# Two transposes of the routing four units later, and the exponential two units earlier, in a one-core transformer kernel

## The chip, the cores and the metric

The kernel is one launch on one core of a Trainium2 chip. The metric is device time in microseconds of that core. A core has five engines with a program of their own each, which meet only through semaphores: TensorE (PE in the profile), VectorE (DVE), ScalarE (ACT), GpSimd (POOL) and SyncE (SP), which here only issues the loads.

## The reference, cut to what matters

Two blocks run one after the other on 256 tokens of width 1024: a transformer block with two layers, then a block with a state-space branch, an attention branch and a PEER layer, all in fp32. The change is in the PEER layer. It is:

```
q = (x @ w_q)                       # 8 heads, 2 halves of 128
s1, s2 = q . sub_k1, q . sub_k2     # 128 scores per head and half
v1, i1 = top_k(s1, 16); v2, i2 = top_k(s2, 16)
cand_s = v1[..., :, None] + v2[..., None, :]        # 16 x 16
top_s, pos = top_k(cand_s, 16)
experts = (i1 * 128 + i2) at pos;  gates = softmax(top_s)
act = gelu(u_tab[experts] . x) * gates
out = sum_e act * v_tab[experts]
```

There are 128 x 128 experts and each token takes 8 x 16 of them.

## The kernel before, in words

The kernel does not gather experts. It computes the hidden value of every expert for every token, multiplies it with a gate that is zero where the token did not choose the expert, and multiplies the result with the whole second table. The first table is streamed as 128 *expert units* (stage `ut`, 512 KB each, 128 experts), the second as 128 more (stage `vt`).

A weight tile of fp32 is split in two halves so that TensorE's faster number format can be used with three products: ScalarE copies the tile to `wh` (L845), and VectorE or GpSimd subtracts to get `wl` (L1121, L1709). Which of the two does it stands in the list `lower`: for `ut` it is GpSimd below the unit `J_GATE` and VectorE from there on. There are four slots, so a unit's halves can be made only when the unit four before it has been used by TensorE. At its place j each engine's program makes the half of unit j + 3 at the latest (`stream`, `until`).

The order of work is written out by hand, as a loop over j from 0 to 127 in each engine's program:

- **TensorE**: `hidden(j)`, 24 products of 128 x 256, into one of four banks. Ahead of unit 25 and of unit 51 (`J_SEL`) stands `sel_turned(t)` (L782): it waits until VectorE has finished the routing of token tile t (event `picked`) and transposes three tiles, gates (`gt`) and the two chosen indices (`sel`), into bank 2 or 3. From `J_GATE` = 53 on, for 64 units, `gates_of(j - J_GATE)` (L791) adds, for four tokens each, the product of two one-hot matrices: the gates of four tokens for all experts.
- **ScalarE**: the exponential of `gt` of tile t ahead of its unit 25 or 51 (it waits for the event `top`), then `wh`, then the Gelu of `hidden(j)`; in the gate phase also a copy of gates into `H` for the units that are still to come.
- **VectorE**: `routing(t)` (L1594) is a generator that is moved on by one step at each j, by two where j % 5 is 4: 16 steps of a top-16 over 128 scores, 8 of a top-16 over 256 sums, the subtraction that gives `top`, index arithmetic, four wide operations and two sums over 128 x 2048, and the softmax's last product (`picked`). At j = 25 and 51 what is left of it is done at once, then `sel_turned(t)` (L1626) copies the transposed tiles from the bank, then the next tile's routing starts. From j = 53 on it makes the one-hot matrices (`one_hots`), nine in rotation, multiplies the gates into `H` for the units already computed (`gates_in`, width 4 x (J_GATE + g + 1)), and gates the new unit (`gated_hidden`).
- **GpSimd**: only `wl`.

Each call `wait_ge` in this code issues an instruction only if the engine has not met that value already.

Of the kernel before, what the change touches and what calls it, by code (L numbers as in the profile page):

```python
# [95 lines left out]
def program(nc, x_d, pos_d, consts_d, smalls_d, win_d, wout_d, wup_d, wdown_d, rows_d, wu_d, wqkv_d, wqk_d, wga_d, wsm_d,  # L96
            wglu_d, wsu_d, wau_d, wout2_d, wpq_d, keys_d, ut_d, vt_d, out_d, spill_d):
    with ExitStack() as ctx:
# [51 lines left out]
        def signal(name, step=1):  # L150
            return Signal(ctx.enter_context(nc.semaphore(name)), name, step)

        pe_out, act_out, dve_out, pool_out = [signal(n) for n in ("pe_out", "act_out", "dve_out", "pool_out")]
# [57 lines left out]


        J_SEL = (25, 51)
        J_GATE, N_GR = 53, 64


        lower = []
# [157 lines left out]
        def RT(n):  # L375
            r_at[0] += n
            assert r_at[0] <= 32768
            return H_s[:, r_at[0] - n:r_at[0]]
# [12 lines left out]
        sel = RT(256).rearrange("p (a n) -> p a n", a=2)  # L391
# [9 lines left out]
        def gate_bank(g):  # L401
            return (2, 3, 6, 7)[g % 4]

        def hid_bank(j):
            return (0, 1, 4, 5)[j % 4]

        def gated_before(j):
            return min(max(j - J_GATE, 0), N_GR)
# [36 lines left out]
        def pe(p):  # L445
# [7 lines left out]
            def claim(b):  # L453
                if emptied[b]:
                    p.wait_ge(emptied[b][0], *emptied[b][1:])
# [318 lines left out]
            def hidden(j):  # L774
                i, b = first["ut"] + j, hid_bank(j)
                unit(i)
                claim(b)
                m = mm3(banks[b][:, 0:256], [unit_pair(i, k, 8, tcols(0)) for k in range(8)], [hT(k, ALLC) for k in range(8)], True, True, ready_both(("f", 2)))
                m.then_inc(pe_out.up(("used", i), ("hid", j)), 1)
                emptied[b] = (dve_out, ("HG", j)) if gated_before(j) else (act_out, ("H", j))  # L780

            def sel_turned(t):  # L782
                b = 2 + t
                claim(b)
                p.wait_ge(dve_out, ("picked", t))
                for j, src in enumerate((gt.rearrange("p h k -> p (h k)"), sel[:, 0, :], sel[:, 1, :])):
                    m = p.e.transpose(banks[b][:, j * 128:(j + 1) * 128], src, ids[:, :])
                m.then_inc(pe_out.up(("sel", t)), 1)
                emptied[b] = (dve_out, ("selG", t))

            def gates_of(g):  # L791
                b = gate_bank(g)
                claim(b)
                for t in range(4):
                    k = 4 * g + t
                    p.wait_ge(dve_out, ("oh", k))
                    o = oneh[k % N_OH]
                    mm(banks[b][:, t * 128:(t + 1) * 128], [(o[:, 0, :], o[:, 1, :])]
                       ).then_inc(pe_out.up(("Gt", k), ("G", g) if t == 3 else None), 1)
                emptied[b] = (dve_out, ("G", g))  # L800
# [17 lines left out]
                                m.then_inc(pe_out.up(("Vend", t)), 1)  # L818

            for j in range(128):  # L820
                if j in J_SEL:
                    sel_turned(J_SEL.index(j))
                hidden(j)
                if 0 <= j - J_GATE < N_GR:
                    gates_of(j - J_GATE)
# [5 lines left out]
        def act(a):  # L831
# [5 lines left out]
            def stream(i):  # L837
                while at[0] <= until[i]:
                    u = at[0]
                    at[0] += 1  # L840
                    if plan[u][2]:
                        a.wait_ge(slot_in[slot[u]], ("raw", u))
                        if halves_of[u] is not None:
                            a.wait_ge(pe_out, ("used", halves_of[u]))
                        a.e.activation(high_of(u), raw_of(u), ACTF.Copy).then_inc(act_hi.up(("hi", u)), 1)  # L845

            def do(out, src, f, ev, **kw):
                a.e.activation(out, src, f, **kw).then_inc(act_out.up(ev), 1)  # L848
# [218 lines left out]
            stream(first["keys"])  # L1067
            stream(first["keys"] + 1)
            for j in range(128):
                if j in J_SEL:  # L1070
                    t = J_SEL.index(j)
                    a.wait_ge(dve_out, ("top", t))
                    do(gt, gt, ACTF.Exp, ("gt", t))
                stream(first["ut"] + j)

                n, b = 4 * gated_before(j), hid_bank(j)
                a.wait_ge(pe_out, ("hid", j))
                if j * 256 + 256 > R_AT:
                    a.wait_ge(dve_out, ("selG", 1))
                if n < 256:  # L1080
                    do(H[:, j, n:256], banks[b][:, n:256], ACTF.Gelu_apprx_tanh, ("H", j))
                if n:
                    do(banks[b][:, 0:n], banks[b][:, 0:n], ACTF.Gelu_apprx_tanh, ("H", j))
                g = j - J_GATE
                if 0 <= g < N_GR:
                    a.wait_ge(pe_out, ("G", g))
                    do(H[:, j + 1:128, 4 * g:4 * g + 4], banks[gate_bank(g)][:, :].rearrange("p (t j) -> p j t", t=4)[:, j + 1:128, :],
                       ACTF.Copy, ("Gs", g))
# [23 lines left out]
        def dve(v):  # L1112
# [11 lines left out]
            def tt(out, a, b, op, ev=None, alone=False):  # L1124
                if not alone:
                    v.wait_ge(dve_out)
                v.e.tensor_tensor(out, a, b, op).then_inc(dve_out.up(ev), 1)  # L1127
# [177 lines left out]
            for L in range(DEPTH):  # L1305
# [76 lines left out]
                for n in range(2):  # L1382
                    for h in range(4):
                        if h in (0, 3):
                            t = h // 3
# [155 lines left out]
            for c in range(20):  # L1541
# [4 lines left out]
                if c - 4 in (7, 15):  # L1546
                    t = (c - 4) // 8
# [9 lines left out]
            for n in range(2):  # L1557
                for h in range(4):
                    if h in (0, 3):
                        t = h // 3  # L1560
# [33 lines left out]
            def routing(t):  # L1594
                v.wait_ge(act_out, ("S", t, 12))
                for n in range(16):
                    top16(v16[:, n, :], i16[:, n, :], S[:, t, n, :])
                    yield
                vv = v16.rearrange("p (h c) k -> p h c k", c=2)
                tt(cand.rearrange("p h (i j) -> p h i j", i=16), vv[:, :, 0, :].unsqueeze(3).broadcast_to([128, 8, 16, 16]),  # L1600
                   vv[:, :, 1, :].unsqueeze(2).broadcast_to([128, 8, 16, 16]), ALU.add)
                for h in range(8):
                    top16(tops[:, h, :], pos[:, h, :], cand[:, h, :])
                    yield
                tt(gt, tops, tops[:, :, 0:1].broadcast_to([128, 8, 16]), ALU.subtract, ("top", t))
                posf_ = pos.rearrange("p h k -> p (h k)")
                ts(pau, posf_, 4, None, ALU.logical_shift_right, None)
                ts(pbu, posf_, 15, None, ALU.bitwise_and, None)
                copy(pa, pau)
                copy(pb, pbu)  # L1610
                copy(if16, i16)
                yield
                ifv = if16.rearrange("p (h c) k -> p h c k", c=2)
                for c, pp in ((0, pa), (1, pb)):
                    tt(oh, pp.rearrange("p (h k) -> p h k", h=8).unsqueeze(3).broadcast_to([128, 8, 16, 16]),
                       iot.unsqueeze(1).unsqueeze(1).broadcast_to([128, 8, 16, 16]), ALU.is_equal)
                    yield
                    tt(oh, oh, ifv[:, :, c, :].unsqueeze(2).broadcast_to([128, 8, 16, 16]), ALU.mult)
                    reduce_sum(sel[:, c, :].rearrange("p (h k) -> p h k", h=8), oh)
                    yield  # L1620
                v.wait_ge(act_out, ("gt", t))
                reduce_sum(zs, gt)
                reciprocal(zs, zs)
                tt(gt, gt, zs.unsqueeze(2).broadcast_to([128, 8, 16]), ALU.mult, ("picked", t))

            def sel_turned(t):  # L1626
                bank = banks[2 + t]
                v.wait_ge(pe_out, ("sel", t))
                v.wait_ge(spilled, "spill")
                copy(sel1[:, tcols(t)], bank[:, 128:256])  # L1630
                copy(sel2[:, tcols(t)], bank[:, 256:384])
                copy(selG[:, tcols(t)], bank[:, 0:128], ("selG", t))
# [24 lines left out]
            for j in range(128):  # L1657
                if j in J_SEL:
                    for _ in steps:
                        pass  # L1660
                    sel_turned(J_SEL.index(j))
                    steps = routing(1) if j == J_SEL[0] else iter(())
                next(steps, None)
                if j % 5 == 4:
                    next(steps, None)
                g = j - J_GATE
                if 0 <= g < N_GR:
                    one_hots(g)
                stream(first["ut"] + j - (g >= 0))
                if 0 < g <= N_GR:  # L1670
                    gates_in(g - 1)
                gated_hidden(j - 1)
# [310 lines left out]
```

## Time and profile before

| | |
|---|---|
| Median of 3 runs | 1963.02 us (1962.67 to 1963.16) |
| The profiled execution | 1962.71 us, of which 1960.6 us is the span from its first to its last instruction |
| TensorE busy | 1785.2 us (91%) |
| VectorE busy | 1281.3 us (65%) |
| ScalarE busy | 868.9 us (44%) |
| GpSimd busy | 779.2 us (40%) |
| Mean granted TensorE clock | 0.925 |

The profile is of one execution. A line such as "PE bank L468" in it names an engine, the tile that is written and the line of the program; "idle before" is the time that the engine stood still ahead of the instruction, and the arrow names what released it. Because helpers issue most instructions, L468 stands for nearly all products, L787 for the six transposes of `sel_turned`, L848 for ScalarE's functions, L1127 for VectorE's operations on two tensors. The routing of the PEER layer lies between about 1155 and 1320 us of the span, its gate phase between about 1331 and 1566 us, and the second table after about 1597 us.

### The profile page before, as it was taken

Reading aid. Unit: us, or ns where it says so; the run is one execution under the profiler, and the core shown is the slowest. Engines: PE = TensorE matmul, PEld = TensorE weight load, DVE = VectorE, ACT = ScalarE, POOL = GpSimd, SP = SyncE. Lnnn points to the kernel's source line nnn. Section 1 sums busy time; section 2 is a strip of 40 time slices with the busy share of each in tenths; the row PEclk is TensorE's granted clock in tenths of the full one; section 3 lists DMA queues with packets and bytes.
Section 4 is the critical chain, followed back from the end, with each engine's and each line's share of the span. In section 5 each row is a group of like instructions: output and inputs, shape, how many; then the busy total and the mean of one; then the engine's idle time right before and its main releaser. Section 6 shows DMA issues by size and latency. Waiting matters only on the chain.

```text
span 1960.6 us, 27291 instructions
## 1 busy us (share of the span) xinstructions
PE 1785.2 (91%) x10680; PEld 1555.1 (79%) x10680; DVE 1281.3 (65%) x2470; ACT 868.9 (44%) x1500; POOL 779.2 (40%) x410
## 2 busy tenths in 40 slices
PE   5999899789989997688889899789999999999997
PEld 4677899677669996555667799789999988888886
DVE  6653674954546758687763459998999944444444
ACT  5443565335336652412432344444444445555553
POOL 3211468432125683175633359770000014444443
PEclk9887899899789998788967899899999999999998
DMA  6421455444115554322321535454444456666664
GB/s 219 140 76 33 167 179 192 145 175 133 54 36 201 181 175 161 132 76 76 105 77 54 179 127 182 149 166 142 144 141 141 149 170 193 194 195 193 194 192 141
DMA packets 77311, 283.19 MB, mean 144 GB/s; under 512 B 8704, under 2 KB 8960, under 8 KB 76800
## 3 DMA queue, kind: packets, MB, share of 16 engines
q1 hardware_dynamic: 75888, 275.97, 43.3%
q10 hardware_dynamic: 1296, 5.49, 0.7%
q8 instruction: 84, 1.38, 0.3%
q14 instruction: 43, 0.35, 0.1%
HBM read 279.33 MB, written 2.10 MB: 144 GB/s over the span
## 4 chain that ended last, share of the span: by engine, by line
PE 64%; DVE 24%; ACT 4%; issue 4%; POOL 3%; DMA 1%; POOLq 0%; DVEq 0%; ACTq 0%
PE bank L468 52%; PE bank L459 9%; DVE wl L1121 4%; DVE tab L1127 2%; DVE H L1127 2%; ACT wh L845 2%; PE bank L551 2%; DVE att L1132 2%; DVE ssb L1127 1%; DVE att L1138 1%; DVE H L1586 1%; DVE H L1592 1%; DVE H L1588 1%; DVE H L1584 1%; DVE H L1590 1%
## 5 line engine op out<-in xcount | busy, mean ns | idle before, releaser
L1709 POOL TENSOR_TENSOR wl<-raw,wh 128x1024 fp32r<-128x1024 f32 x231 | 598.9, 2602 | 862.3 <-ACT wh L845 862.1
L845 ACT ACTIVATE wh<-raw 128x1024 fp32r<-128x1024 f32 x515 | 531.4, 1048 | 175.4 <-PE bank L468 166.0
L468 PE MATMUL bank<-hh,wh 128*128 128x256 f32 x1904 | 545.6, 287 | 18.6 <-DVE hl L1127 17.3
L468 PE MATMUL bank<-hl,wh 128*128 128x256 f32 x1904 | 538.1, 283 | 0.0
L468 PE MATMUL bank<-hh,wl 128*128 128x256 f32 x1904 | 536.8, 282 | 0.0
L1121 DVE TENSOR_TENSOR wl<-raw,wh 128x1024 fp32r<-128x1024 f32 x284 | 402.7, 1426 | 131.0 <-ACT wh L845 130.8
L468 PEld LDWEIGHTS bank<-hh,wh 128*128 128x128 f32 x1904 | 364.4, 191 | 20.9 <-issue 14.4
L468 PEld LDWEIGHTS bank<-hl,wh 128*128 128x128 f32 x1904 | 364.3, 191 | 0.0
L468 PEld LDWEIGHTS bank<-hh,wl 128*128 128x128 f32 x1904 | 363.8, 191 | 0.0
L1127 DVE TENSOR_TENSOR acl<-H,ach 128x256 fp32r<-128x256 f32 x128 | 87.6, 685 | 183.2 <-ACT ach L848 183.2
L468 PE MATMUL bank<-wh,ach 128*128 128x512 f32 x512 | 200.0, 391 | 1.9 <-DVE acl L1127 1.9
L468 PE MATMUL bank<-wl,ach 128*128 128x512 f32 x512 | 199.9, 390 | 0.0
L468 PE MATMUL bank<-wh,acl 128*128 128x512 f32 x512 | 199.7, 390 | 0.0
L468 PE MATMUL bank<-wh,hh 128*128 128x512 f32 (+1 forms) x432 | 184.3, 427 | 11.5 <-DVE hl L1127 6.6
L848 ACT ACTIVATE H<-bank 128x256 f32<-128x256 f32 (+33 forms) x193 | 63.8, 331 | 256.5 <-PE bank L468 224.0
L468 PE MATMUL bank<-wl,hh 128*128 128x512 f32 (+1 forms) x432 | 177.2, 410 | 0.0
L468 PE MATMUL bank<-wh,hl 128*128 128x512 f32 (+1 forms) x432 | 176.8, 409 | 0.0
L848 ACT ACTIVATE ach<-H 128x256 fp32r<-128x256 f32 x128 | 53.4, 418 | 174.3 <-PE bank L468 173.8
L1138 DVE SCALAR_TENSOR_TENSOR att<-bank,sml,att 128x255 f32<-128x255 f32 (+1 forms) x176 | 84.5, 480 | 64.0 <-ACT att L848 60.9
L468 PEld LDWEIGHTS bank<-wh,hh 128*128 128x128 f32 x432 | 88.1, 204 | 41.0 <-issue 15.2
L468 PEld LDWEIGHTS bank<-wh,ach 128*128 128x128 f32 x512 | 96.4, 188 | 22.3 <-issue 2.1
L468 PEld LDWEIGHTS bank<-wl,ach 128*128 128x128 f32 x512 | 96.5, 189 | 20.1
(183 smaller groups left out, 2439.5 us busy)
## 6 DMA issues: line engine op xcount, KB each, us to landing
raw<-in_ut_dram SPq DMA_DIRECT2D x128, 512.0 KB, 3.5
raw<-in_vt_dram SPq DMA_DIRECT2D x128, 512.0 KB, 3.6
raw<-in_wup_dram SPq DMA_DIRECT2D x88, 512.0 KB, 4.0
raw<-in_win_dram SPq DMA_DIRECT2D x48, 512.0 KB, 4.5
raw<-in_wdown_dram SPq DMA_DIRECT2D x44, 512.0 KB, 3.6
raw<-in_wout_dram SPq DMA_DIRECT2D x24, 512.0 KB, 3.5
raw<-in_wga_dram SPq DMA_DIRECT2D x16, 512.0 KB, 3.6
raw<-in_wpq_dram SPq DMA_DIRECT2D x16, 512.0 KB, 3.6
```

The lines of the kernel that those rows point to most:

```text
L459: m = p.e.matmul(out, l, r, start=i == 0, stop=i == len(pairs) - 1)
L468: m = p.e.matmul(out, lhs[i][a], rhs[i][b], start=start and i == 0 and j == 0, stop=stop and i == n - 1 and j == 2)
L551: m = p.e.transpose(banks[b][:, 128 * k:128 * k + 128], buf[:, 1024 + 256 * (i % NB) + 128 * k:1152 + 256 * (i % NB) + 128 * k], ids[:, :])
L845: a.e.activation(high_of(u), raw_of(u), ACTF.Copy).then_inc(act_hi.up(("hi", u)), 1)
L848: a.e.activation(out, src, f, **kw).then_inc(act_out.up(ev), 1)
L1121: v.e.tensor_tensor(low_of(u), raw_of(u), high_of(u).bitcast(F32), ALU.subtract).then_inc(dve_lo.up(("lo", u)), 1)
L1127: v.e.tensor_tensor(out, a, b, op).then_inc(dve_out.up(ev), 1)
L1132: v.e.tensor_scalar(out, a, s1, None, op0).then_inc(dve_out.up(ev), 1)
L1138: v.e.scalar_tensor_tensor(out, a, s, b, op0, op1).then_inc(dve_out.up(ev), 1)
L1584: v.e.max(values[:, 0:8], s_).then_inc(dve_out.up(), 1)
L1586: v.e.max_index(index[:, 0:8], values[:, 0:8], s_).then_inc(dve_out.up(), 1)
L1709: g.e.tensor_tensor(low_of(u), raw_of(u), high_of(u).bitcast(F32), ALU.subtract).then_inc(pool_lo.up(("lo", u)), 1)
```

## The change

In TensorE's and VectorE's loops `sel_turned(t)` stands at units 29 and 55 instead of 25 and 51, and the gate phase begins at unit 57 instead of 53 (so units 53 to 56 of `ut` are lowered by GpSimd, not VectorE, and `gates_in` is 16 elements wider each time). ScalarE's exponential stands at units 23 and 49 instead of 25 and 51. VectorE still finishes tile 0's routing and starts tile 1's at unit 25. A wait is written ahead of the subtraction that overwrites `gt`.

```
-        J_GATE, N_GR = 53, 64
+        J_TURN = (29, 55)
+        J_GATE, N_GR = 57, 64
 (TensorE)
-                if j in J_SEL:
-                    sel_turned(J_SEL.index(j))
+                if j in J_TURN:
+                    sel_turned(J_TURN.index(j))
                 hidden(j)
 (ScalarE)
-                if j in J_SEL:
-                    t = J_SEL.index(j)
+                if j + 2 in J_SEL:
+                    t = J_SEL.index(j + 2)
                     a.wait_ge(dve_out, ("top", t))
                     do(gt, gt, ACTF.Exp, ("gt", t))
 (VectorE, routing)
+                if t:
+                    v.wait_ge(pe_out, ("sel", t - 1))
                 tt(gt, tops, tops[:, :, 0:1].broadcast_to([128, 8, 16]), ALU.subtract, ("top", t))
 (VectorE, loop)
                 if j in J_SEL:
                     for _ in steps:
                         pass
-                    sel_turned(J_SEL.index(j))
                     steps = routing(1) if j == J_SEL[0] else iter(())
+                if j in J_TURN:
+                    sel_turned(J_TURN.index(j))
```

## Rows read from the trace of the kernel before

**Rows 1.** The page's chain that ended last, shares of the span by engine

```profile
PE 64%; DVE 24%; ACT 4%; issue 4%; POOL 3%; DMA 1%; POOLq 0%; DVEq 0%; ACTq 0%
```

**Rows 2.** Waits of TensorE, 1000 to 1700 us: total us, times, longest

```profile
PE bank L787 <- DVE H L1127: 18.0, 2, 10.0
```

**Rows 3.** TensorE in order of time (start us, us, what)

```profile
1237.14 0.87 PE L787 MATMUL bank<-ids,H 128*128 128x128 f32 x3 [9.96 <-DVE H L1127]
1237.67 0.56 PE L468 MATMUL bank<-hh,wh 128*128 128x256 f32 x1
...
1320.22 0.90 PE L787 MATMUL bank<-ids,H 128*128 128x128 f32 x3 [8.07 <-DVE H L1127]
1320.77 0.56 PE L468 MATMUL bank<-hh,wh 128*128 128x256 f32 x1
...
1326.04 0.34 PE L468 MATMUL bank<-hh,wh 128*128 128x256 f32 x1
```

**Rows 4.** Windows: stretch, us, busy PE, PEld, DVE, ACT, POOL; clock, DMA share, GB/s

```profile
1250.00:1312.00 62.00, 62.00 (x533) 61.94 (x531) 58.52 (x156) 29.33 (x44) 56.72 (x22) 1.00 0.56 179
1480.00:1520.00 40.00, 40.00 (x349) 40.00 (x348) 40.00 (x119) 18.12 (x44) 0.00 (x0) 1.00 0.41 137
```

**Rows 5.** ScalarE in order of time around its units 25 and 51

```profile
1227.22 0.38 ACT L848 ACTIVATE H<-bank 128x256 f32<-128x256 f32 x1 [1.46 <-PE bank L468]
1227.62 1.28 ACT L848 ACT_TABLE_LOAD   x1
...
1230.19 1.28 ACT L848 ACT_TABLE_LOAD   x1
1242.18 0.39 ACT L848 ACTIVATE H<-bank 128x256 f32<-128x256 f32 x1 [10.71 <-PE bank L468]
...
1312.18 0.38 ACT L848 ACTIVATE H<-bank 128x256 f32<-128x256 f32 x1 [1.47 <-PE bank L468]
...
1326.28 0.39 ACT L848 ACTIVATE H<-bank 128x256 f32<-128x256 f32 x1 [9.84 <-PE bank L468]
```

**Rows 6.** VectorE in order of time, both routings

```profile
1208.52 0.29 DVE L1127 TENSOR_TENSOR H<-H 128x128 f32<-128x128 f32 x1
...
1235.32 1.67 DVE L1127 TENSOR_TENSOR H<-H 128x128 f32<-128x128 f32 x1
1238.05 0.94 DVE L1143 COPY xs<-bank 128x128 f32<-128x128 f32 x3 [1.06 <-PE bank L787]
1239.03 0.29 DVE L1584 MAX8 H<-H 128x8 f32<-128x128 f32 x1
...
1268.55 2.29 DVE L1127 TENSOR_TENSOR H<-H 128x2048 f32<-128x2048 f32 x1
...
1290.95 0.29 DVE L1127 TENSOR_TENSOR H<-H 128x128 f32<-128x128 f32 x1
...
1319.87 0.29 DVE L1127 TENSOR_TENSOR H<-H 128x128 f32<-128x128 f32 x1
```

**Rows 7.** GpSimd in order of time: lower halves, one unit each

```profile
1225.80 4.39 POOL L1709 TENSOR_TENSOR wl<-raw,wh 128x1024 fp32r<-128x1024 f32 x1
1230.15 4.40 POOL L1709 TENSOR_TENSOR wl<-raw,wh 128x1024 fp32r<-128x1024 f32 x1
1234.51 2.34 POOL L1709 TENSOR_TENSOR wl<-raw,wh 128x1024 fp32r<-128x1024 f32 x1
...
1296.79 2.40 POOL L1709 TENSOR_TENSOR wl<-raw,wh 128x1024 fp32r<-128x1024 f32 x1 [0.32 <-ACT wh L845]
```

**Rows 8.** VectorE and TensorE in order of time, gate phase

```profile
1481.11 0.78 DVE L1127 TENSOR_TENSOR H<-H,bank 128x376 f32<-128x376 f32 x2
...
1561.79 0.36 PE L468 MATMUL bank<-hh,wh 128*128 128x256 f32 x1
...
1561.84 0.35 DVE L1641 TENSOR_SCALAR xs<-sta,xs 128x128 f32<-128x128 bf16 x1
...
1566.07 0.97 DVE L1127 TENSOR_TENSOR H<-H,bank 128x468 f32<-128x468 f32 x2 [0.74 <-ACT H L848]
```

## The prediction

> **What bounds the kernel now.** I read the page's chain first: TensorE carries 64% of it and VectorE 24% [rows 1], so a gain must come from time in which TensorE stands still or runs slow. The waits of TensorE in the last third then have one large entry: the transposes of `sel_turned` waited 18.0 us for VectorE, in two waits, the longer 10.0 us [rows 2]. In order of time these are 9.96 us ahead of unit 25 and 8.07 us ahead of unit 51 [rows 3]. Between them TensorE is busy 62.00 of 62 us at full granted clock [rows 4]: nothing else holds it.
>
> The true price of a stall is larger than its wait, since TensorE resumes at the low clock. ScalarE's Gelus follow TensorE's units, so their distance tells it. From Gelu 25 at 1242.18 to Gelu 50 at 1312.18 are 25 units in 70.0 us, 2.80 us each [rows 5]. Gelu 24 to Gelu 25 took 14.96 us, so stall 25 cost 12.16 us; Gelu 50 to Gelu 51 took 14.10, so stall 51 cost 11.30 us [rows 5]. Together 23.46 us. The slow part can be seen: unit 51 ran from 1320.77 to 1326.04, 5.27 us instead of 2.80 [rows 3], 2.5 us at 1.2 instead of 2.4 GHz for most of it; unit 25 started at 1237.67 [rows 3] and its Gelu came 4.5 us later [rows 5], so about 1.6 us.
>
> Why is VectorE late? Its routing of tile 1 starts at 1239.03 and its last product ends at 1319.87 + 0.29 = 1320.16 [rows 6]: 81.1 us of almost unbroken work. The 26 units of TensorE that are meant to cover it take 26 x 2.80 = 72.8 us. So VectorE's routing, not TensorE, sets when unit 51 starts, and that is the number on which the change has to be judged.
>
> **The change, first tile.** Tile 0's routing ends at 1235.32 + 1.67 = 1236.99 [rows 6]. Without the stall TensorE would go on after unit 24 (about 1226.95) with units 25 to 28, 11.2 us, to 1238.15, already past 1236.99. But GpSimd must have made their lower halves. In front of each of the last ones it takes turns with VectorE's wide operations: the three operations that start at 1225.80, 1230.15 and 1234.51 are the halves of units 26, 27 and 28, and end at 1230.19, 1234.55 and 1236.85 [rows 7] (the last one started before the stall ended belongs to unit 28, the last that `stream(25)` allows). Unit 26 would start at 1229.75 and so waits 0.4 us; unit 27 would start at 1233.0 and waits 1.6 us; unit 28 runs 1237.4 to 1240.2. So `sel_turned(0)` is reached at about 1240.2 and finds `picked` long set: no stall for VectorE, 2.0 us for GpSimd, and 0.5 us for the transposes themselves (1237.14 to 1237.67 [rows 3]). The two short waits may lower the clock for one unit, which costs 0 to 2.5 us by unit 51's row; I take 0. As shown next, it drops out of the sum in either case.
>
> **The change, second tile.** VectorE no longer stands for TensorE's transposes after tile 0 and starts tile 1 at 1237.0 instead of 1239.03, 2.04 us sooner. Its three copies (0.94 us [rows 6]) come at its unit 29, four steps into the routing; their transposes are then long done. So VectorE is 2.04 - 0.94 = 1.10 us ahead, and tile 1 is picked at about 1320.16 - 1.1 = 1319.1. TensorE runs from 1240.75 with units 29 to 54, 72.8 us, and reaches `sel_turned(1)` at 1313.5. It waits 5.6 us. This is where the first tile's 0 to 2.5 us vanish: they only shorten this wait. TensorE then pays transposes and a slow first unit as before; I take the same 2.5 us (bounds: 0, if the shorter idle leaves the clock up, and 2.5 as now, with 1.6 of unit 25 between).
>
> **The sum.** Before, unit 51 starts 0.61 us after `picked`, at 1320.77 [rows 3, 6]. After, unit 55 starts 0.6 us after `picked`, at about 1319.7. So at a moment 1.1 us earlier, four more units are done. All units, all 64 gate steps and all 128 units of the second table are still to be done in both, and TensorE was the bound in them, so the four units are the gain: 4 x 2.80 + 1.10 = 12.3 us. Counted from the other side: 23.46 us lost before, 2.0 + 0.5 + 5.6 + 0.6 + 2.5 = 11.2 us lost after, difference 12.3.
>
> **What costs nothing, and its cover.** The wait ahead of the `gt` subtraction: VectorE has met the same event in its own copies at unit 29, so it issues no instruction. The earlier exponential: at unit 23 `top` of tile 0 is set at 1208.81 [rows 6], over 10 us ahead; at unit 49 ScalarE comes at about 1296.9, and `top` of tile 1, 1291.24 less 1.1 [rows 6], is there 6 us before. What is queued behind it is the high half of unit 26 (52) and a Gelu. From the end of one Gelu at 1227.60 to the end of the second table load at 1231.47 ScalarE spends 3.87 us including one high half of about 1.05, so the exponential with its two loads costs 2.8 us [rows 5], now beside a running TensorE. ScalarE idles 1.47 us per unit [rows 5], so it is level again after two units, and the high half is four units ahead of its use. Price if the cover is gone: at most 2.8 us ahead of unit 29 or 55, again only taken from the waits there. The Trainium skill, "ScalarE: Activation LUTs", section "What ACT_TABLE_LOAD costs", gives a load of 1283 ns plus a drain of 1380 ns for every switch, and so speaks against moving the switches beside running work: an estimate of 5.6 us by it instead of 2.8. The trace has the load (1.28 us) but no drain ahead of it (Gelu ends 1227.60, load starts 1227.62), so the row is used; by the page's figure too the result would stay, as ScalarE's delay ends in the wait at unit 55.
>
> The gate phase: TensorE and VectorE are both busy 40.00 of 40 us in 1480 to 1520 [rows 4], so VectorE is close to taking over. `gates_in` grows by 16 elements a step. The pair of operations grew from 0.78 us (376 + 160 elements) to 0.97 (468 + 252) [rows 8], 1.03 ns an element; 64 x 16 x 1.03 = 1.06 us in all. VectorE's last one-hot of the phase ends at 1562.19, when TensorE has just begun the unit ahead of its last gate step (1561.79 + 2.8) [rows 8]: 2.4 us in hand, of which at most 1.06 goes. Cost 0; bounds 0 and 1. GpSimd lowers four units more (53 to 56) in time that it had free; VectorE saves them, but after the stall.
>
> **A size I can't fix: turns with GpSimd.** VectorE's wide operation took 2.29 us at 1268.55 [rows 6], and GpSimd's took 4.39 where both were wide and 2.34 to 2.40 alone [rows 7]. So one turn is worth about 2.1 us. In the new order tile 1's candidate sum comes within 0.1 us of GpSimd's next start, and the exponential delays GpSimd's unit 52 just where VectorE's wide operations begin (1296.9 [rows 7]). VectorE may lose or win a turn. A lost one at the candidate sum is mostly given back at the index arithmetic, which waits for the same GpSimd end. I take 0, and -2.1 and +2.8 us (one whole unit later) as ends.
>
> **The rivals.** (a) *Both stalls go*, 23.5 us, 1939.6 us: needs VectorE to route a tile in 72.8 us; it needs 81.1, and nothing of it is removed. 3%. (b) *VectorE wins a turn, or the clock stays up at unit 55*: 12.3 + 2.3, 1948.4 us. 13%. (c) *VectorE loses a turn in tile 1*: `picked` 2.8 us later, 1953.5 us. 13%. (d) *Little is gained*: the four units run, but GpSimd, which shares its turns with VectorE, holds TensorE for more than I count and pushes VectorE as well, three turns, 6 to 8 us: 1958. 4%. (e) *Slower*: VectorE becomes the bound of the gate phase. Its place is each of the 64 steps; it decides once VectorE's step is longer than TensorE's unit plus gates by over 12.3/64 = 0.19 us on the mean. The last steps are some 0.1 us longer now, so a strided write that costs more than its elements would be needed. At 0.25 us a step, 16 us, so 3.7 slower: 1966.7 us. 4%. (f) *It does not do what it says*: TensorE stands at unit 29 for something else as long as at 25: 1963. 3%.
>
> **How the numbers follow.** The forecast has 60%. Against the profiled execution, 1962.71 us (span 1960.6 and 2.11 around it), it is 1950.4; the median of the runs is 0.31 higher, so 1950.7 us. Its own range is 1949.2 to 1952.3. For 8 in 10 the range takes in (b) and (c): 1947.5 to 1954.5. A difference of 0.2% (4 us) is about what can be told here: faster 0.92 (forecast, a, b, c and most of d), same 0.04, slower 0.04.
>
> **What would show it.** No wait of the transposes at unit 29; short waits of TensorE for `wl` L1709 of 0.4 and 1.6 us near 1230 and 1233; one wait at unit 55 of 5 to 6 us for VectorE's last product, with low clock behind it; tile 1's routing starting at 1237; the gate phase still at TensorE's pace. It is wrong if unit 55 starts later than 1322, or if waits for one-hots appear in the gate phase.

## The result, and the profile after

| | before | after |
|---|---|---|
| Median of 20 runs each | 1961.13 us (1947.05 to 1971.12) | 1941.28 us (1931.87 to 1959.17) |
| Ratio of the runs | | 0.9927 (95%: 0.9900 to 0.9955) |
| The profiled execution | 1962.71 us, span 1960.6 | 1932.87 us, span 1930.8 |
| Mean granted clock | 0.925 | 0.938 |

The kernel is faster, and the predicted ratio, 1950.7 / 1963.02 = 0.9937, lies in the interval. The predicted time does not hold: the median is 9.4 us below it and 6.2 below the range. The ratios here and below leave out single runs over 1.5% above the fastest of their kernel, one each in three of the later comparisons. The two profiled executions differ by 29.8 us in span, far more than the 12.3 us of the prediction. So there are two questions: what did the change do, and where are the other 17 us?

The waits of TensorE in the last third, after the change (total us, times, longest), which answer to [rows 2]:

```profile
PE bank L788 <- DVE H L1128: 5.7, 1, 5.7
PE bank L469 <- POOL wl L1713: 2.9, 3, 1.3
PE bank L469 <- DVE acl L1128: 1.9, 1, 1.9
```

One wait for VectorE is left, 5.7 us; 5.6 was forecast. TensorE in order of time, which answers to [rows 3]: the unit that waits for GpSimd's half, the transposes of tile 1, and the first product of the second table.

```profile
1142.17 0.39 PE L469 MATMUL bank<-hh,wh 128*128 128x256 f32 x1 [1.28 <-POOL wl L1713]
...
1217.30 0.38 PE L469 MATMUL bank<-hh,wh 128*128 128x256 f32 x1 [1.32 <-POOL wl L1713]
...
1302.04 0.90 PE L788 MATMUL bank<-ids,H 128*128 128x128 f32 x3 [5.74 <-DVE H L1128]
1302.60 0.56 PE L469 MATMUL bank<-hh,wh 128*128 128x256 f32 x1
...
1568.72 0.47 PE L469 MATMUL bank<-wh,ach 128*128 128x512 f32 x1 [1.91 <-DVE acl L1128]
```

The first and the last row bound a stretch that can be compared: from unit 1, which in both kernels waits 1.28 us for its half, to the second table. It takes 1568.72 - 1142.17 = 426.55 us. In the kernel before these two rows are:

```profile
1159.43 0.39 PE L468 MATMUL bank<-hh,wh 128*128 128x256 f32 x1 [1.28 <-POOL wl L1709]
...
1598.44 0.47 PE L468 MATMUL bank<-wh,ach 128*128 128x512 f32 x1 [1.91 <-DVE acl L1127]
```

That is 439.01 us. The change took 12.46 us from the stretch it touches. The other 17.3 us were gained before unit 1 began, in code that is the same in both kernels: 15.7 of them in the attention steps of the first block's layer 0, and 1.8 in those of layer 1 (table below). Windows of the attention steps of the first block's layer 0 (stretch, us, busy PE, PEld, DVE, ACT, POOL, granted clock, DMA share, GB/s), first of before, then of after:

```profile
131.00:154.00 23.00, 23.00 (x79) 16.85 (x78) 9.43 (x41) 8.14 (x32) 2.50 (x2) 0.51 0.08 24
154.00:171.00 17.00, 16.44 (x66) 12.58 (x65) 6.34 (x19) 5.39 (x16) 0.00 (x0) 0.56 0.01 1
```

```profile
131.00:154.00 23.00, 21.64 (x137) 16.67 (x136) 13.80 (x57) 12.63 (x46) 1.08 (x2) 1.00 0.08 25
```

The column to read is the clock, 0.51 against 1.00: TensorE ran the same instructions at 1.2 GHz in the one execution and at 2.4 in the other, and got 79 or 137 of them done in 23 us. TensorE looks fully busy in the slow one, which is why a list of waits does not show this loss. The mean granted clock of the single runs goes with their time as well: among the 20 runs after the change it is 0.938 in the fastest (1931.87 us) and 0.923 in the slowest (1959.17 us).

### The profile page after: what moved, and what is told of

Read it like the earlier page. It is cut to its first block, busy times and chain, and to the rows that moved or that the text cites. A ratio compares the mean times of both kernels' runs of the same rounds, so it can differ in the third digit from the quotient of the medians.

```text
span 1930.8 us, 27287 instructions
## 1 busy us (share of the span) xinstructions
PE 1764.5 (91%) x10680; PEld 1540.3 (80%) x10680; DVE 1272.1 (66%) x2462; ACT 867.7 (45%) x1500; POOL 789.6 (41%) x414
## 3 DMA queue, kind: packets, MB, share of 16 engines
q8 instruction: 84, 1.38, 0.3%
## 4 chain that ended last, share of the span: by engine, by line
PE 63%; DVE 25%; ACT 4%; issue 4%; POOL 3%; DMA 1%; POOLq 0%; DVEq 0%; ACTq 0%
PE bank L469 52%; PE bank L460 8%; DVE wl L1122 4%; DVE tab L1128 2%; DVE H L1128 2%; ACT wh L846 2%; PE bank L552 2%; DVE att L1133 2%; DVE ssb L1128 1%; DVE att L1139 1%; DVE H L1587 1%; DVE H L1593 1%; DVE H L1589 1%; DVE H L1591 1%; DVE H L1585 1%
## 5 line engine op out<-in xcount | busy, mean ns | idle before, releaser
L1713 POOL TENSOR_TENSOR wl<-raw,wh 128x1024 fp32r<-128x1024 f32 x235 | 609.0, 2603 | 821.2 <-ACT wh L846 821.0
L469 PE MATMUL bank<-hh,wh 128*128 128x256 f32 x1904 | 546.0, 287 | 20.2 <-DVE hl L1128 17.3
L1122 DVE TENSOR_TENSOR wl<-raw,wh 128x1024 fp32r<-128x1024 f32 x280 | 396.3, 1423 | 129.2 <-ACT wh L846 129.0
L469 PEld LDWEIGHTS bank<-wl,ach 128*128 128x128 f32 x512 | 96.6, 189 | 20.2
```

The lines of the kernel that those rows point to most:

```text
L469: m = p.e.matmul(out, lhs[i][a], rhs[i][b], start=start and i == 0 and j == 0, stop=stop and i == n - 1 and j == 2)
L1122: v.e.tensor_tensor(low_of(u), raw_of(u), high_of(u).bitcast(F32), ALU.subtract).then_inc(dve_lo.up(("lo", u)), 1)
L1713: g.e.tensor_tensor(low_of(u), raw_of(u), high_of(u).bitcast(F32), ALU.subtract).then_inc(pool_lo.up(("lo", u)), 1)
```

## The experiments

For every profiled execution I read the same marks from TensorE's order. *Layer 0* is from its third group of q and k transposes to the transposes of the normed rows that wait 6.0 us; *layer 1* the same in the next layer; *stretch* is the one above. Each row is one profiled execution; the ratio is that of all its kernel's runs to runs of the kernel before in the same comparison.

| kernel | ratio (95%) | layer 0 | layer 1 | to unit 1 | stretch |
|---|---|---|---|---|---|
| before | | 88.3 | 88.7 | 1159.4 | 439.0 |
| before, look 1 | | 72.6 | 86.9 | 1140.1 | 436.7 |
| before, look 2 | | 88.3 | 88.6 | 1162.4 | 436.8 |
| before, look 3 | | 72.6 | 87.0 | 1147.0 | 436.5 |
| after | 0.9927 (0.9900 to 0.9955) | 72.6 | 86.9 | 1142.2 | 426.6 |
| after, again | 0.9936 (0.9908 to 0.9964) | 88.3 | 88.7 | 1159.5 | 425.7 |
| first move only | 0.9975 (0.9944 to 1.0007) | 72.6 | 87.0 | 1149.4 | 433.6 |
| second move only | 0.9946 (0.9922 to 0.9969) | 88.3 | 88.7 | 1162.2 | 430.5 |
| exponential back | 0.9958 (0.9922 to 0.9995) | 90.2 | 87.0 | 1168.5 | 426.4 |
| transposes at 29 and 58 | 0.9899 (0.9853 to 0.9944) | 88.4 | 86.8 | 1157.3 | 421.0 |
| the same, again | 0.9907 (0.9871 to 0.9943) | 88.3 | 88.7 | 1162.4 | 420.6 |

Layer 0 is not the only part ahead of unit 1 that varies. From the end of *layer 1* to unit 1 these eleven executions took between 571.5 us (look 1) and 581.0 us (first move only), in the same code. So look 1 reached unit 1 6.9 us before look 3, with layers 0 and 1 alike. Where in that part the 9.5 us lie was not worked out.

### The changed kernel again

No edit.

> The changed kernel once more, unaltered. Theory A (the change gains 12.4 us in the stretch of the first expert table, all of it where it was worked out, and the rest of the difference between the two profiles is the granted clock of the first block's attention steps, which is drawn anew in each execution): from the first product of unit 1 to the first product of the second table 426.5 us again (before 439.0), the attention steps of the two layers (about 24 us each at full clock, about 40 us at the low one) at either clock in this profile, single runs spread over some 25 us, and over many rounds a ratio of about 0.9937 (12.4 of 1960). Theory B (the change itself keeps the clock up in the first block, by code placement or the like): both attention stages as in the profile after, layer 0 at full clock, and a ratio of about 0.985 with little spread.

Stretch 425.7 us, layer 0 at the low clock this time, span 1947.4. Over its runs the ratio is 0.9936. Theory A holds: an unaltered kernel drew the other clock, 15.7 us longer in layer 0, and reached unit 1 17.4 us later than in its first profile. Its single runs spread over 18.6 us, not 25.

### Three looks at the kernel before

No edit.

> The kernel before, unaltered, for another look at one execution. Theory A (layer 0's attention steps run at full or at low clock by a draw in each execution of every kernel): the stage from the third transpose of q and k (near 113 us) to that of the normed rows takes 72.6 or 88.3 us here, and in at least one of three such looks 72.6; the stretch of the first expert table takes 439.0 us in all three. Rival (the full clock there comes with the change): 88.3 us in all three.

> As the look before it: 72.6 or 88.3 us in layer 0's stage by a draw, 439.0 us in the expert stretch; the rival has 88.3 us here too.

> As the two looks before it: 72.6 or 88.3 us in layer 0's stage by a draw, 439.0 us in the expert stretch; the rival has 88.3 us here too.

Two of the three had layer 0 at 72.6 us, so the full clock is not the change's doing. What decides between the two levels no run shows. Look 1 ran in 1939.5 us altogether, faster than the predicted time of the faster kernel. The windows of looks 1 and 2:

```profile
131.00:154.00 23.00, 21.62 (x137) 16.65 (x136) 13.79 (x57) 12.63 (x46) 1.05 (x2) 1.00 0.08 25
```

```profile
131.00:154.00 23.00, 23.00 (x79) 16.74 (x79) 9.38 (x41) 8.14 (x32) 2.67 (x2) 0.52 0.07 24
```

The stretch was expected at 439.0 and is 436.5 to 436.8. The wait at unit 51 is shorter by one of VectorE's turns with GpSimd (look 1):

```profile
1299.22 0.90 PE L787 MATMUL bank<-ids,H 128*128 128x128 f32 x3 [5.53 <-DVE H L1127]
```

against 8.07 in [rows 3]. In look 1 VectorE's first wide operation of tile 1's indices took 2.29 us (1277.99), where the first profile has 4.42: it came before GpSimd's, which started at 1278.18, not after. In the first profile it is this row, behind GpSimd's of 1296.79 in [rows 7]:

```profile
1296.92 4.42 DVE L1127 TENSOR_TENSOR H<-H,sta 128x2048 f32<-128x2048 f32 x1
```

In looks 2 and 3 it also took 2.29 us. So the kernel before has two lengths of this stretch, its first profile had the longer, seen once in four, and the mean gain is some 11 us, not the 12.5 of the first pair. Against the three looks alone it is 10.5.

### Only the first tile's transposes moved

```
-        J_TURN = (29, 55)
-        J_GATE, N_GR = 57, 64
+        J_TURN = (29, 51)
+        J_GATE, N_GR = 53, 64
```

> The transposes of tile 0 stand at unit 29, those of tile 1 back at 51, and the gate phase back at 53; the earlier exponentials stay. Theory A (VectorE's two routings in a row set when tile 1 is picked, so a stall removed at the first tile comes back at the second): no wait at unit 29, a wait at unit 51 of about 5.6 + 4 x 2.8 = 16.8 us, unit 1 to second table about 439.0 - 1.1 = 437.9 us, ratio 0.999 to 1.000. Rival (each stall is a cost of its own, so that the first one's 12.2 us go with its move): about 427 us and ratio 0.994.

The wait at unit 29 is gone and the one at unit 51 has grown:

```profile
PE bank L788 <- DVE H L1128: 12.7, 1, 12.7
```

It is 12.7 us, not 16.8, and the stretch 433.6, between the two theories but nearer to A (437.9) than to the rival (427). Against the 436.6 us of the three looks the first move alone is worth 3.0 us, so most of the 9.96 us stall does come back. The 4 us are VectorE's turns. Its wide operations of tile 1 here, then in the changed kernel:

```profile
1297.46 2.29 DVE L1128 TENSOR_TENSOR H<-H,sta 128x2048 f32<-128x2048 f32 x1
1299.79 2.29 DVE L1128 TENSOR_TENSOR H<-H 128x2048 f32<-128x2048 f32 x1
```

```profile
1289.87 4.42 DVE L1128 TENSOR_TENSOR H<-H,sta 128x2048 f32<-128x2048 f32 x1
1294.33 4.38 DVE L1128 TENSOR_TENSOR H<-H 128x2048 f32<-128x2048 f32 x1
```

Here GpSimd has nothing to do any more: its last unit is 52, since VectorE lowers from 53 on, and it ended at 1292.96:

```profile
1290.17 2.79 POOL L1713 TENSOR_TENSOR wl<-raw,wh 128x1024 fp32r<-128x1024 f32 x1 [1.96 <-ACT wh L846]
```

Two turns, 2 x 2.1 us, are not waited for, and tile 1 is picked that much earlier. In the changed kernel GpSimd also lowers units 53 to 56, beside these operations. That units go to the other engine was costed at nothing in the prediction; beside the routing they cost VectorE these two turns, some 4 us. Whether VectorE could have lowered them for less, no run shows.

### Only the second tile's transposes moved

```
-        J_TURN = (29, 55)
+        J_TURN = (25, 55)
```

> The transposes of tile 0 back at unit 25, those of tile 1 at 55, the gate phase at 57 as in the changed kernel. Theory A: the 10 us stall at unit 25 stays with its slow unit, TensorE reaches unit 55 at about tile 1's end (30 units x 2.8 after 1239.3 = 1323.3 in the time of the kernel before, tile 1 picked at 1320.2), so there is no wait at 55, and all but 1.1 us of the gain is here: 439.0 - 11.3 = 427.7 us from unit 1 to the second table, ratio about 0.994. Rival (each stall its own, the gain of the changed kernel comes from the first): not more than the second stall's difference of 11.3 - 8.7 = 2.6 us, 436 us, ratio 0.999.

```profile
PE bank L788 <- DVE H L1128: 9.9, 1, 9.9
PE bank L469 <- POOL wl L1713: 2.9, 3, 1.3
```

One wait of 9.9 us at unit 25, none at 55. The stretch is 430.5 us: 2.8 above theory A's 427.7, but clearly below the rival's 436. Short waits for lower halves, 0.31 and 1.32 us ahead of units 51 and 52, now appear for tile 1, and the transposes' 0.55 us are still paid; I had counted neither. So each move alone is worth something: 5.4 and 8.5 us against the first profile, and 12.5 together. Against the three looks it is 3.0, 6.1 and 10.5. By the first the two give less together than one by one, by the second more; which profile of the kernel before is taken decides it, so neither is shown.

### The exponential back at units 25 and 51

```
-                if j + 2 in J_SEL:
-                    t = J_SEL.index(j + 2)
+                if j in J_SEL:
+                    t = J_SEL.index(j)
```

> The changed kernel with the exponentials back at units 25 and 51. Theory A (the earlier exponential is worth nothing, since it ends far ahead of VectorE's sums at both places): stretch from unit 1's product to the second table 426.1 us (425.7 and 426.6 so far), waits for lower halves 0.3 and 1.3 us as before, ratio 0.9936. Rival (moving it is a cost or a gain by its two table loads, 2.8 us each, or by a turn of GpSimd won or lost): 422 to 429 us.

426.4 us, between the changed kernel's two values; the rival's 422 to 429 take it in too, but nothing of its 2.8 us or of a turn is to be seen. Of the short waits the one of 1.3 us is there and the one of 0.3 is not. The earlier exponential is worth nothing here, to within 1 us. ScalarE around it in the changed kernel:

```profile
1204.27 0.38 ACT L849 ACTIVATE H<-bank 128x256 f32<-128x256 f32 x1 [1.46 <-PE bank L469]
1204.67 1.28 ACT L849 ACT_TABLE_LOAD   x1
1205.97 0.31 ACT L849 ACTIVATE H<-H 128x128 f32<-128x128 f32 x1
1206.18 1.04 ACT L846 ACTIVATE wh<-raw 128x1024 fp32r<-128x1024 f32 x1
1207.25 1.28 ACT L849 ACT_TABLE_LOAD   x1
1208.54 0.39 ACT L849 ACTIVATE H<-bank 128x256 f32<-128x256 f32 x1
```

Each load starts within 0.03 us of the end of what is ahead of it, as in [rows 5]; no further 1.38 us a switch, the drain that the Trainium skill names in "ScalarE: Activation LUTs", section "What ACT_TABLE_LOAD costs", can be seen.

### The transposes at 29 and 58, the gate phase at 60

```
-        J_TURN = (29, 55)
-        J_GATE, N_GR = 57, 64
+        J_TURN = (29, 58)
+        J_GATE, N_GR = 60, 64
```

> The transposes of tile 1 at unit 58 and the gate phase at 60, tile 0's at 29. Theory A: the wait of 5.7 us at unit 55 goes, with its slow unit (2.5 us): TensorE reaches unit 58 some 2.8 us after tile 1 is picked. Unit 1 to second table 426.5 - 5.7 - 2.5 = 418.3 us, ratio to the kernel before 0.9895. The gate phase ends at unit 123, VectorE's reserve there shrinks by at most 64 x 12 x 1.03 ns = 0.8 us of about 2, so no wait for one-hots. Rival (VectorE becomes the bound of the gate phase once it starts later and each step is wider): waits for one-hots near the end of the gate phase and 421 us or more.

> The kernel with the transposes at units 29 and 58 and the gate phase at 60 again, since its first comparison rested on 6 runs. From the traces so far its stretch is 421 us, 18.1 less than before, so 0.9908; the rival is that a part of this is given back in other stages, then 0.9935 or more, the ratio of the changed kernel.

```profile
PE bank L469 <- POOL wl L1713: 4.2, 4, 1.3
PE bank L469 <- DVE acl L1128: 1.9, 1, 1.9
```

No wait for VectorE's routing is left, and no wait for one-hots. Windows of the late gate phase:

```profile
1480.00:1560.00 80.00, 80.00 (x695) 80.00 (x693) 80.00 (x234) 35.23 (x86) 0.00 (x0) 1.00 0.41 139
```

VectorE is busy all the time, and TensorE too: the reserve was enough. The stretch is 421.0 and 420.6 us, not 418.3: GpSimd's two short waits (1.6 us) come for tile 1 as well, and the rest, about 1 us, stays open. The rival had named 421 us, but its mechanism, waits for one-hots, did not come. The stretch is 5.4 us shorter than that of the changed kernel and about 16 to 18 shorter than before. Over the runs this version is clearly faster than the kernel before; that it beats the changed kernel is shown by the stretch alone, as the intervals of the ratios overlap. The second comparison, 0.9907, agrees with the 0.9908 worked out from the first profile, and as well with the 0.992 that the three looks would give.

### Products meant to hold the clock

After each of the last 20 attention steps of both layers one product more, never read, or two:

```
+                claim(6)
                 for c in range(24, N_ATT + 4):
                     att_step(c)
+                    p.e.matmul(banks[6][:, 0:128], ids[:, :], ids[:, :], start=True, stop=True)
```

> The kernel before, with one product of the identity by itself (128 x 128, never read) into the idle bank 6 after each of the 20 attention steps that follow the last input slab, in both layers of the first block. Theory A (the spread of the single runs and most of the miss is TensorE's granted clock in these steps, which falls or stays by chance in layer 0: 42.2 or 57.9 us from the third transpose of q and k to that of the mix): if full-width products keep the clock up, both layers take about 42.2 + 20 x 0.22 = 46.6 us each in every execution, 10 us less than now in layer 1, and the single runs lie closer together; ratio about 0.993. If they do not, the stages are 20 x 0.44 = 8.8 us longer at the low clock, ratio about 1.006. Rival (the spread comes from elsewhere, DMA or the later stages): spread of the single runs as before.

> The same 20 products per layer in the kernel with the transposes at units 29 and 58. Theory A: gains add, as the stages are apart: expert stretch 421 us, layers 0 and 1 of attention at 46.6 us, ratio 0.990 x 0.993 = 0.983. If the products do not hold the clock: 0.996.

> Two such products per step. Theory A: where one is enough, this is 20 x 2 x 0.22 = 8.8 us slower than one, ratio 0.987; where one is too little to hold the clock, two may do it: layers 51 us each, ratio about 0.987 also, against 0.996 for one.

In the kernel before: ratio 1.0073 (1.0028 to 1.0117), layer 0 96.7 us and layer 1 95.1, that is 8.4 and 6.4 us more at the low clock. In the kernel with 29 and 58 one product gives 0.9972 (0.9926 to 1.0019) with 96.6 and 95.1 us, two give 1.0014 (0.9971 to 1.0058) with 81.0 and 102.6. In the last one layer 0 ran 8.4 us above its short length, layer 1 14 us above its long one. Neither one nor two products hold the clock in layer 1; the idea fails, and this way costs. In layer 0 it stays open, as each clock was seen without them too. The single runs did not move closer together: they lay in two groups, 1956.5 to 1958.1 and 1981.4 to 1986.7 us for the first. What sets the groups apart is not shown, since no profile of that kernel fell in the lower one.

## Why the prediction was right on the gain and wrong on the time

**What bounds the kernel.** Right. The two stalls of [rows 2] and [rows 3] were the place, and VectorE's routing of tile 1 the bound. The experiment with the first move alone shows it: the stall comes back at unit 51. The measured median, 1941.3 us, lies next to rival (a), both stalls gone, 1939.6 us; yet the wait at unit 55 was there, so that nearness is chance.

**First tile.** Right: no wait for VectorE at unit 29, waits for lower halves of 0.3 and 1.32 us where 0.4 and 1.6 were worked out from [rows 7]. They left the clock up, as taken: the 24 products behind the longer one took 2.91 us, where 2.80 is the full clock's.

**Second tile.** Wait 5.74 us for 5.6 forecast; 5.73 in the repeat. Twenty of the products behind it ran at the low clock (12 in the repeat), so that unit 55 took 4.94 us (4.19), which is 2.1 us (1.4) over the full clock's 2.80, for the 2.5 taken.

**The sum.** 12.3 us forecast, 12.46 between the profiled pair, 10 to 13 over all pairs of looks. That the first pair agrees to 0.2 us is partly luck: the rows of the forecast and this pair share the one profile of before with the longer stretch, and the other three give 10.5. The turns with GpSimd, named as a size that could not be fixed, moved as well: in the changed kernel the candidate sum lost its turn (4.34 us for 2.29 in [rows 6]) and the first wide operation won one (2.29 for 4.42), so they cancelled against that profile. Against the looks, where the kernel before has won that turn too, the change loses one in tile 1, the mechanism of rival (c). The gate phase cost nothing, as forecast, and rivals (a), (d), (e) and (f) did not come. The units 53 to 56 that went to GpSimd were taken as free; the experiment with the first move shows that they cost VectorE up to two turns. It did not spoil the sum, which was worked out with as many turns in tile 1 as the first profile had.

**How the numbers follow.** This is the step that failed. It took the level from one profiled execution and three runs that lay within 0.5 us of each other, and the range from the bounds of the stretch alone. The rest of the program, some 1500 us, was taken to repeat. It does not: layer 0's attention steps have two lengths, 72.6 and 88.3 us, in both kernels, the part between layer 1 and unit 1 varies by 9.5 us more, and in the eleven executions of the table unit 1 was reached between 1140 and 1168 us. The profile of before had layer 0 at the long one.

The miss of 9.4 us can be split. The kernel before ran in 1959.2 us on the mean of its 20 runs, not in 1963.0: 3.8 us. The means of the two kernels lie 14.2 us apart (1959.2 and 1945.0), not 12.3: 1.9 us, well inside the noise of that comparison. And the median after lies below the mean: 11 of the 20 runs took at most 1941.3 us, the next one 1947.5: 3.7 us. How far a median moves by such draws can be seen from the kernel before itself, whose median was 1961.1, 1960.4, 1952.0 and 1952.0 us in four comparisons. They were not all made on one chip, which may have a part in that; but looks 1 and 2 came from one chip and still lay 23.6 us apart.

The sign could have been seen in the profile at hand: a stage of 40 us with TensorE 96 to 100% busy at a granted clock of 0.51 to 0.57, in layer 0 and again in layer 1 (515 to 554 us). The windows of the execution after show that layer 0's needs about 24 us at full clock. Against its own comparison the change did what was worked out (0.9927, then 0.9936, for 0.9937 forecast), though intervals of 0.3% either way would have taken in 10 or 14 us as well. The time, as a figure in microseconds, needed a range wider by the 15.7 us of layer 0 alone, which also makes the 4 us named as the least that can be told too small for single runs.

## What to carry to other kernels

A stall that is set by a chain on another engine is hardly removed at its first occurrence (3 to 5 us of 12 here): most of its price comes back where the chain ends, and the gain is the work that is put ahead of that end. Here that was four units of 2.8 us, and three more gave half as much again before the chain was covered. Before forecasting a time, look for stretches in which the matrix engine is fully busy at the low clock. Such a stretch may come out the other way in the next execution, as layer 0 did here and layer 1 did not, and no list of waits names it. Take several executions of the kernel before as the base, and forecast the difference rather than the time.

## What the runs showed of the hardware

- The granted clock of a stage can settle at either level in executions of the same program: 40 us at 0.51 to 0.56 or about 24 us at 1.00 for layer 0's attention steps. In layer 1 the low level came in all eleven executions (86.8 to 88.7 us). Its small products follow each other without a wait at the low clock.
- After a wait of 5.5 to 12.7 us TensorE ran 12 to 24 products of 256 columns at the low clock; in the same kernel 12 in one execution and 20 in another. After a wait of 1.32 us it ran none.
- VectorE's operation on two 128 x 2048 tensors took 2.29 us, or mostly 4.3 to 4.4 beside GpSimd, so what one GpSimd instruction more or less in the neighbourhood costs is a whole turn of 2.1 us. The first sum over 128 x 2048 elements took 2.29 us in every routing, also where GpSimd was busy beside it.
